# Six of eight chunks of an MLP up projection computed as Strassen products of quarters

## The chip, the cores and the metric

The kernel runs on one core of one Trainium2 chip. The metric is the device time of one execution in microseconds (us). TensorE does the matmuls, VectorE, ScalarE and GpSimd the elementwise work, and SyncE issues loads. The engines run side by side and wait for each other through semaphores.

## The reference, cut to what matters

The program computes one layer of an encoder: a mixer, a cross-attention and a squared-ReLU MLP. All but the MLP's first half is left as it is.

```
D_MODEL, SEQ, D_FF = 2048, 512, 8192
def squared_relu_mlp(h, w_up, w_down):
    u = jax.nn.relu(jnp.einsum('bsd,df->bsf', h, w_up))
    return jnp.einsum('bsf,fd->bsd', u * u, w_down)
...
x = x + squared_relu_mlp(rms_norm(x, ln_mlp), w_mlp_up, w_mlp_down)
```

## The kernel before

All matmuls are in pairs of fp32r parts: a value is `hi` (rounded on ScalarE) plus `lo` (the rest, by a subtraction on VectorE), and a product of two values is three matmuls, hi by hi, hi by lo, lo by hi (`hi_lo`, lines 867 to 869).

The up projection of the MLP has D_FF = 8192 columns, in 64 slabs of 128 columns, eight to a chunk (`MC`), eight chunks (`NCH`). A slab is 2048x128 weights: 1 MB, held as 128x2048 in `w_raw`, two buffers. Its 16 blocks of 128x128 are the stationary operand, the 512 tokens of `act_hi` and `act_lo` the moving one: 16 x 3 matmuls of 512 columns into one bank `slab_ps` (`window`). SyncE loads `w_raw` as soon as the split of the slab two before is done. ScalarE makes `w_hi` (`split_hi`, L1491), VectorE `w_lo` (`split_lo`, L2096). After a slab VectorE takes the ReLU and scales it (`hidden_relu`, L2792, into `urelu`), ScalarE squares it into `ucomb` (`hidden_square`, L1962). After two slabs GpSimd makes four sums of 128x256 out of the squares (`sum_hidden`, L813 to L816: the down projection is already done as Strassen products, and these are its activation sums). ScalarE and VectorE split the seven operands (`u_hi` L1970, `u_lo` L2799, 128x1792), and GpSimd's queue parks both in DRAM (`park_hidden`, `u_park`). In slabs 1 to 4 of the first chunk TensorE also transposes `main`, the residual, 16 blocks in each (`main_turns`, L1428), and ScalarE and VectorE copy them back.

Every engine's queue is in the order in which its code is written (`up_chunk` on ScalarE and on VectorE, `window` on TensorE, `sum_hidden` and `park_hidden` on GpSimd), and an instruction that waits holds up all behind it. Chunks 1 to 6 are a loop. Then the down projection follows, with `half_hi` (L2008) and `half_lo` (L2834) as its weight splits and `t` as its weight sums, all 128x1024.

## Time and profile before

| | |
|---|---|
| time, three executions | 2875.32, 2876.81, 2878.39 us, median 2876.81 |
| span of the profiled execution | 2873.9 us, from its first to its last instruction |
| the profiled execution's own time | not given apart from its span |
| busy: TensorE, VectorE, ScalarE, GpSimd | 2837.2, 1653.3, 1060.7, 405.2 us |
| ReLUs of the up projection, first and last | 1553.8 and 2245.0 us of the span |

A busy time counts the span from the start to the modelled end of an engine's instructions. Matmuls are pipelined, so that the time of one as shown is longer than the distance from its start to the next one's; the distance is what a row of them costs. Ends on VectorE and ScalarE overlap the next start a little too. An instruction's idle time before it stands in brackets, with what ended it.

### The profile page before, as it was taken

What the parts mean: (1) busy time and instruction counts of PE and PEld (TensorE: products, weight loads), DVE (VectorE), ACT (ScalarE), POOL (GpSimd) and SP (SyncE); (2) the same over time, 40 slices, a digit from 0 to 9 for tenths busy, and PEclk for the clock granted to TensorE, in tenths of its full rate; (3) what the DMA queues carried; (4) which work ended last, traced back from release to release, by engine and by line L of the source; (5) the groups of instructions that cost most, each with busy time, mean ns of one, the idle gap of its engine ahead of it and who ended that gap; (6) DMA issues with size and microseconds to landing.
All of it is one profiled execution on the core that took longest, in us unless ns stands there. A gap on an engine that the chain in (4) does not pass through costs nothing.

```text
span 2873.9 us, 38425 instructions
## 1 busy us (share of the span) xinstructions
PE 2837.2 (99%) x14896; PEld 2372.4 (83%) x14896; DVE 1653.3 (58%) x1699; ACT 1060.7 (37%) x1155; POOL 405.2 (14%) x438
## 2 busy tenths in 40 slices
PE   8999999999999999999999999999999999999997
PEld 5888777788899988898888888888888888888886
DVE  7545777755454433534534433333343798888888
ACT  5433433423453322332424322323233333333334
POOL 4000000000001132200011233233233200000001
PEclk9999999999999999999999999999999999999999
DMA  5333232233357764423423555556556755556555
GB/s 166 97 85 87 75 82 63 68 91 81 107 145 233 218 201 121 176 88 105 145 74 88 165 184 186 177 174 195 179 166 203 270 219 219 208 215 218 205 211 132
DMA packets 453647, 439.80 MB, mean 153 GB/s; under 512 B 9104, under 2 KB 365488, under 8 KB 453424
## 3 DMA queue, kind: packets, MB, share of 16 engines
q1 hardware_dynamic: 424288, 344.56, 39.1%
q0 software_dynamic: 29264, 93.90, 9.2%
q8 instruction: 68, 1.11, 0.2%
...
## 4 chain that ended last, share of the span: by engine, by line
PE 89%; DVE 5%; ACT 2%; DMA 2%; issue 2%; POOL 0%; DVEq 0%; SPq 0%; ACTq 0%
PE slab_ps L867 18%; PE slab_ps L869 18%; PE slab_ps L868 18%; PE down_ps L1465 6%; PE down_ps L1467 6%; PE down_ps L1466 6%; PE mix_ps L869 2%; PE mix_ps L868 2%; PE mix_ps L867 2%; PE down_ps L867 2%; PE down_ps L869 2%; PE down_ps L868 2%; DVE dn_c L2246 1%; ACT w_hi L1491 1%; DMA w_raw<-in_w_in_dram 1%
## 5 line engine op out<-in xcount | busy, mean ns | idle before, releaser
L867 PE MATMUL slab_ps<-act_hi,w_hi 128*128 128x512 f32 (+2 forms) x2704 | 1022.6, 378 | 15.1 <-DVE act_lo L2148 11.2
L868 PE MATMUL slab_ps<-act_lo,w_hi 128*128 128x512 f32 (+2 forms) x2704 | 999.8, 370 | 0.0
L869 PE MATMUL slab_ps<-act_hi,w_lo 128*128 128x512 f32 (+2 forms) x2704 | 999.8, 370 | 0.0
L2096 DVE TENSOR_TENSOR w_lo<-w_raw,w_hi 128x2048 fp32r<-128x2048 f32 x200 | 469.2, 2346 | 370.7 <-ACT w_hi L1491 370.0
L867 PEld LDWEIGHTS slab_ps<-act_hi,w_hi 128*128 128x128 f32 (+1 forms) x2704 | 509.5, 188 | 109.6 <-issue 23.4
L869 PEld LDWEIGHTS slab_ps<-act_hi,w_lo 128*128 128x128 f32 (+1 forms) x2704 | 509.2, 188 | 87.9 <-issue 0.8
L868 PEld LDWEIGHTS slab_ps<-act_lo,w_hi 128*128 128x128 f32 (+1 forms) x2704 | 509.8, 189 | 85.0 <-issue 5.1
L1491 ACT ACTIVATE w_hi<-w_raw 128x2048 fp32r<-128x2048 f32 x200 | 381.9, 1910 | 476.1 <-PE slab_ps L869 359.8
L1465 PE MATMUL down_ps<-half_hi,u_slot 128*128 128x512 f32 x896 | 349.5, 390 | 0.8 <-DMA u_slot<-u_park 0.8
L1467 PE MATMUL down_ps<-half_lo,u_slot 128*128 128x512 f32 x896 | 349.5, 390 | 0.0
L1466 PE MATMUL down_ps<-half_hi,u_slot 128*128 128x512 f32 x896 | 349.3, 390 | 0.0
L1962 ACT ACTIVATE ucomb<-urelu 128x512 f32<-128x512 f32 x64 | 40.5, 633 | 485.0 <-DVE urelu L2792 485.0
L2008 ACT ACTIVATE half_hi<-t 128x1024 fp32r<-128x1024 f32 x128 | 135.7, 1062 | 208.9 <-PE down_ps L1467 159.0
L1465 PEld LDWEIGHTS down_ps<-half_hi,u_slot 128*128 128x128 f32 x896 | 168.3, 188 | 36.9 <-issue 1.2
L2792 DVE SCALAR_TENSOR_TENSOR urelu<-slab_ps,rstd 128x512 f32<-128x512 f32 x64 | 44.3, 692 | 268.1 <-PE slab_ps L869 264.8
L1466 PEld LDWEIGHTS down_ps<-half_hi,u_slot 128*128 128x128 f32 x896 | 168.3, 188 | 35.7
L1467 PEld LDWEIGHTS down_ps<-half_lo,u_slot 128*128 128x128 f32 x896 | 168.3, 188 | 35.6
L2834 DVE TENSOR_TENSOR half_lo<-t,half_hi 128x1024 fp32r<-128x1024 f32 x128 | 157.3, 1230 | 13.8 <-ACT half_hi L2008 12.8
L2008 ACT ACTIVATE half_hi<-b 128x1024 fp32r<-128x1024 f32 x96 | 101.8, 1063 | 149.6 <-PE down_ps L1467 146.1
L2834 DVE TENSOR_TENSOR half_lo<-b,half_hi 128x1024 fp32r<-128x1024 f32 x96 | 117.1, 1221 | 6.5 <-ACT half_hi L2008 6.5
L2101 DVE TENSOR_TENSOR stage<-slab_ps,rstd 128x512 f32<-128x512 f32 (+1 forms) x56 | 38.6, 690 | 111.3 <-PE slab_ps L869 111.1
L2880 DVE TENSOR_TENSOR main<-main,down_ps 128x1024 f32<-128x1024 f32 x64 | 78.1, 1220 | 25.5 <-PE down_ps L1467 25.5
...
## 6 DMA issues: line engine op xcount, KB each, us to landing
w_raw<-in_w_mlp_up_dram SPq DMA_DIRECT2D x64, 1024.0 KB, 6.7
b<-in_w_mlp_down_dram SPq DMA_DIRECT2D x64, 1024.0 KB, 6.9
w_raw<-in_w_in_dram SPq DMA_DIRECT2D x56, 1024.0 KB, 5.6
...
w_raw<-in_w_cross_kv_dram SPq DMA_DIRECT2D x32, 1024.0 KB, 6.3
u_park<-u_hi POOLq DMA_DIRECT2D x32, 896.0 KB, 9.0
u_park<-u_lo POOLq DMA_DIRECT2D x32, 896.0 KB, 8.9
w_raw<-in_w_mix_out_dram SPq DMA_DIRECT2D x16, 1024.0 KB, 5.8
```

What stands on the lines that cost most here:

```text
L867: mm(ps, wh, xh, start=first, stop=False)
L868: mm(ps, wh, xl, start=False, stop=False)
L869: return mm(ps, wl, xh, start=False, stop=last)
L1465: mm(bank[:, t], uh, wh[:, j], start=first, stop=False)
L1466: mm(bank[:, t], ul, wh[:, j], start=False, stop=False)
L1467: ins = mm(bank[:, t], uh, wl[:, j], start=False, stop=last)
L1491: fn(w_hi[:, slot], w_raw[:, slot], ACT.Copy).then_inc(on["slab_hi"], 1)
L2008: fn(half_w[0][h % 4][:], source[q][:, 2 * half:2 * half + 2], ACT.Copy).then_inc(on["slab_hi"], 1)
L2096: tt(w_lo[:, slot], w_raw[:, slot], f32(w_hi[:, slot]), ALU.subtract).then_inc(on["slab_lo"], 1)
L2792: stt(out=urelu[w % 2][:], in0=G[(slabs.first - 1) % 2][:], scalar=0.0, in1=rstd[:], op0=ALU.max, op1=ALU.mult).then_inc(on["slab_out"], 1)
L2834: tt(half_w[1][h % 4][:], source[q][:, 2 * half:2 * half + 2], f32(half_w[0][h % 4][:]), ALU.subtract).then_inc(on["slab_lo"], 1)
L2880: tt(acc[n][q_], acc[n][q_], blocks(bank), ALU.add).then_inc(on["slab_out"], 1)
```

## The change

Chunks 1 to 6 of the up projection are computed in pairs of slabs. The 2048x256 weights of a pair are four quarters of 1024x128 (`b11`, `b12`, `b22`, `b21`, by half of the rows and slab), the activations four quarters of 1024 by 256 tokens. Seven products of one weight operand and one activation operand (`LEFT`) take the place of eight: each 8 x 3 matmuls of 256 columns, added up in three half banks (`joint`, `inner`, `top`).

- SyncE loads four quarters of 512 KB for a pair (`next_quarters`), each as its buffer is freed.
- VectorE makes four weight sums of 128x1024 in a pair (`first_weight_sum` to `fourth_weight_sum`), and seven `w_lo` of 128x1024 (`weight_lo`). ScalarE makes the seven `w_hi` (`weight_hi`). `w_hi` and `w_lo` are rings of four.
- ScalarE copies the bank out after four of the seven products (`part_out`), VectorE adds the parts and takes the ReLU (one operation of 512 columns, five of 256), ScalarE squares. One of the two halves has its sign turned around, and takes the minimum with zero.
- The activation operands are made once, in the first chunk: `left_parts` (ten operations of 128x2048 on VectorE in all) and `left_hi`, `left_lo`, four each. Two of the operands lie where `main` was, so `main` is parked in DRAM before and loaded again in the last chunk, and the transposes move to slabs 3 to 6 of the last chunk. A third lies in a quarter of `act_hi` and `act_lo`; that quarter is parked and loaded again behind product 4 of the last pair, and `returned_window`, the first slab after the pairs, takes its other half first.
- GpSimd's sums of the squares and the parking stay as they are, in numbers and sizes. They lag one pair behind and use one half of `ucomb`, because `t_raw` and one `b12_raw` take the other.

```diff
+        quarter_act = lambda t, i, j: t[:, KT // 2 * j:KT // 2 * (j + 1), HS * i:HS * (i + 1)]
+        ring = lambda w, n: w[:, 1 - n % 4 // 2, n % 2 * (SLAB // 2):(n % 2 + 1) * (SLAB // 2)]
+        LEFT = ([quarter_act(t, 0, 0) for t in (act_hi, act_lo)], [s1[:, part] for part in range(2)],
+                [s24[:, 0, part] for part in range(2)], [s24[:, 1, part] for part in range(2)],
+                [quarter_act(t, 1, 0) for t in (act_hi, act_lo)], [quarter_act(t, 0, 1) for t in (act_hi, act_lo)],
+                [quarter_act(t, 1, 1) for t in (act_hi, act_lo)])
+        left_sum = t1[:].rearrange("p j (a t) -> p (j a) t", t=HS)
+        b11_raw, b22_raw, b21_raw = w_raw[:, 1, 0:SLAB // 2], w_raw[:, 0, 0:SLAB // 2], w_raw[:, 0, SLAB // 2:SLAB]
+        t_raw = ucomb[:, 1, 0:4].rearrange("p a t -> p (a t)")
+        b12_raw = (w_raw[:, 1, SLAB // 2:SLAB], ucomb[:, 1, 4:8].rearrange("p a t -> p (a t)"))
+        weight_raw = lambda n: (b11_raw, t_raw, t_raw, b22_raw, b12_raw[n // STN % 2], b21_raw, t_raw)[n % STN]
+        st_banks = lambda j: (M[j % 2][:, 0:HS], M[2 + j % 2][:, 0:HS], M[4 + j % 2][:, 0:HS])
...
+            def next_quarters(c, j):
+
+                src = quarter_of(c, j + 1, 0, 0)
+                sp.wait_ge(on["slab_lo"], c * (STN * HM) + (ST0 + STN * j + 1))
+                load_quarter(b11_raw, src, raw_in[1])
+                src = quarter_of(c, j + 1, 0, 1)
+                if past_first(c, j > 0):
+                    sp.wait_ge(on["slab_lo"], c * (STN * HM) + (ST0 + STN * (j - 1) + 5))
+                else:
+                    sp.wait_ge(on["u_lo_done"], HM - 1)
+                load_quarter(b12_raw[(j + 1) % 2], src, x_loaded[1])
+                src = quarter_of(c, j + 1, 1, 1)
+                sp.wait_ge(on["slab_lo"], c * (STN * HM) + (ST0 + STN * j + 5))
+                load_quarter(b22_raw, src, raw_in[0])
+                src = quarter_of(c, j + 1, 1, 0)
+                sp.wait_ge(on["slab_lo"], c * (STN * HM) + (ST0 + STN * j + 7))
+                load_quarter(b21_raw, src, x_loaded[0])
...
-            with pe.Fori(1, NCH) as c:
-                slabs.enter(c - 1, MC)
-                for _ in range(MC):
-                    window()
-            slabs.leave(NCH - 1)
+
+            def strassen_pair(c, j):
+
+                joint, inner, top = st_banks(j)
+                for i in range(STN):
+                    n = STN * j + i
+                    pe.wait_ge(on["slab_lo"], c * (STN * HM) + (ST0 + n + 1))
+                    if i == 0 and past_first(c, j >= 2):
+                        pe.wait_ge(on["slab_out"], c * (STN * HM) + (ST0 + STN * j - STN))
+                    if i in (2, 3, 4, 6):
+                        pe.wait_ge(st_copied, c * (4 * HM) + (COPY0 + 4 * j + {2: 1, 3: 2, 4: 3, 6: 4}[i]))
+                    if isinstance(c, int) and c == 0 and j == 0:
+                        if i == 0:
+                            pe.wait_ge(on["x_rstd"], 2)
+                        if i in (1, 2, 3, 4):
+                            pe.wait_ge(on["act_ready"], i + (5 * KT))
+                    wh, wl = (ring(w, n).rearrange("p (k n) -> p k n", n=P) for w in (w_hi, w_lo))
+                    xh, xl = LEFT[i]
+                    bank = (joint, inner, joint, inner, joint, top, joint)[i]
+                    for k in range(KT // 2):
+                        first, end = k == 0 and i in (0, 1, 5), k == KT // 2 - 1
+                        mm(bank, wh[:, k], xh[:, k], start=first, stop=False, skip_group_check=True)
+                        mm(bank, wh[:, k], xl[:, k], start=False, stop=False, skip_group_check=True)
+                        last = mm(bank, wl[:, k], xh[:, k], start=False, stop=end, skip_group_check=True)
+                    last.then_inc(on["slab_mul"], 1)
+
...
+            def left_hi(i):
+                act.wait_ge(st_sums, i + LEFT0)
+                fn(LEFT[i][0], left_sum, ACT.Copy).then_inc(on["xg_hi"], 1)
...
+            def weight_hi(c, n):
+
+                i, j = n % STN, n // STN
+                p = c * HM + (j + 1)
+                if past_first(c, n >= 4):
+                    act.wait_ge(on["slab_mul"], c * (STN * HM) + (ST0 + n - 3))
+                if i in (0, 3, 5):
+                    act.wait_ge({0: raw_in[1], 3: raw_in[0], 5: x_loaded[0]}[i], 16 * p + (16 if i == 5 else RAW0))
+                elif i == 4:
+                    act.wait_ge(st_sums, 4 * (p) + (SUMS0 - 1))
+                elif i == 6:
+                    act.wait_ge(st_sums, 4 * (p) + (SUMS0 - 0))
+                elif i == 1:
+                    act.wait_ge(st_sums, 4 * (p) + (SUMS0 - 3))
+                else:
+                    act.wait_ge(st_sums, 4 * (p) + (SUMS0 - 2))
+                fn(ring(w_hi, n), weight_raw(n), ACT.Copy).then_inc(on["slab_hi"], 1)
...
+            def strassen_pair(c, j, last=False):
+
+                joint, inner, top = st_banks(j)
+                n = STN * j
+                weight_hi(c, n + 3)
+                act.wait_ge(on["u_squared"], c * (2 * HM) + 2 * (HM + j))
+                part_out(c, n, urelu0[:, 0:HS], joint)
+                weight_hi(c, n + 4)
+                part_out(c, n + 1, urelu1[:, HS:S], inner)
+                weight_hi(c, n + 5)
+                part_out(c, n + 2, urelu1[:, 0:HS], joint)
+                weight_hi(c, n + 6)
+                act.wait_ge(on["u_summed"], c * HM + (HM + j))
+                act.wait_ge(on["u_hi_parked"], c * (16 * HM) + 16 * (HM - 1 + j))
+                fn(u_hi[:], ucomb[:, 0, 1:], ACT.Copy).then_inc(on["u_hi_done"], 1)
+                if not last:
+                    weight_hi(c, n + 7)
+                part_out(c, n + 4, urelu0[:, HS:S], joint)
+                if last:
+                    slabs.step(STN * PAIRS - 1)
+                    split_hi(NOT_SLABS, slabs.at(-1))
                     slabs.step()
+                else:
+                    weight_hi(c, n + 8)
+                    weight_hi(c, n + 9)
+                pair_square(c, j, 1)
+                pair_square(c, j, 0)
 
             up_chunk(0, first=True)
-            with act.Fori(1, NCH - 1) as c:
-                slabs.enter(c - 1, MC)
-                up_chunk(c)
-            slabs.leave(NCH - 2)
...
+            def left_parts(i):
+
+                h, l = ([f32(quarter_act(t, *at)) for at in ((0, 0), (0, 1), (1, 0), (1, 1))] for t in (act_hi, act_lo))
+                negated = lambda t: stt(out=left_sum, in0=left_sum, scalar=-1.0, in1=t, op0=ALU.mult, op1=ALU.subtract)
+                plus, minus = ((lambda a, b, op=op: tt(left_sum, a, b, op)) for op in (ALU.add, ALU.subtract))
+                if i == 1:
+                    chain.link(minus(h[3], h[2]))
+                    chain.link(plus(left_sum, l[3]))
+                    minus(left_sum, l[2]).then_inc(st_sums, 1)
+                elif i in (2, 3):
+                    dve.wait_ge(on["act_ready"], i - 1 + (5 * KT))
+                    at = 0 if i == 2 else 1
...
+            def left_lo(i):
+                dve.wait_ge(on["xg_hi"], i + (5 * KT))
+                tt(LEFT[i][1], left_sum, f32(LEFT[i][0]), ALU.subtract).then_inc(on["act_ready"], 1)
...
+                            v.tensor_copy(main[:, 4 * w - 16:4 * w - 12, t * P:(t + 1) * P],
+                                          M[2 + t][:].rearrange("p (k d) -> p k d", d=P)).then_inc(on["main_odd"], 1)
                     if w % 2 and not (first and w == 1):
                         hidden_lo(c, (w - 3) // 2)
+                    if first:
+                        if w in (2, 3, 4):
+                            left_lo(w - 1)
+                        if w <= 4:
+                            left_parts(w)
+                    if not (first and w == MC - 1):
+                        slabs.step()
...
+            def weight_lo(c, n):
+                dve.wait_ge(on["slab_hi"], c * (STN * HM) + (ST0 + n + 1))
+                tt(ring(w_lo, n), weight_raw(n), f32(ring(w_hi, n)), ALU.subtract).then_inc(on["slab_lo"], 1)
...
+            def fourth_weight_sum(c, j):
+
+                dve.wait_ge(x_loaded[0], c * (16 * HM) + 16 * (j + 1) + 16)
+                dve.wait_ge(on["slab_lo"], c * (STN * HM) + (ST0 + STN * j + 3))
+                tt(t_raw, t_raw, b21_raw, ALU.add).then_inc(st_sums, 1)
+
+            def strassen_pair(c, j, last=False):
+
+                joint, inner, top = st_banks(j)
+                n = STN * j
+                product = lambda i: dve.wait_ge(on["slab_mul"], c * (STN * HM) + (ST0 + n + i + 1))
+                copied = lambda i: dve.wait_ge(st_copied, c * (4 * HM) + (COPY0 + 4 * j + i))
+                upper, lower = slice(0, HS), slice(HS, S)
+                third_weight_sum(c, j)
+                weight_lo(c, n + 3)
+                weight_lo(c, n + 4)
+                weight_lo(c, n + 5)
+                fourth_weight_sum(c, j)
+                weight_lo(c, n + 6)
+                dve.wait_ge(on["u_hi_done"], c * HM + (HM + j))
+                dve.wait_ge(on["u_lo_parked"], c * (16 * HM) + 16 * (HM - 1 + j))
+                tt(u_lo[:], ucomb[:, 0, 1:], f32(u_hi[:]), ALU.subtract).then_inc(on["u_lo_done"], 1)
+                product(3)
+                copied(3)
+                tt(urelu1[:, upper], inner, urelu1[:, upper], ALU.add).then_inc(on["slab_out"], 1)
+                if not last:
+                    first_weight_sum(c, j + 1)
+                    weight_lo(c, n + 7)
+                    weight_lo(c, n + 8)
+                    second_weight_sum(c, j + 1)
+                copied(4)
+                tt(urelu1[:, lower], urelu0[:, lower], urelu1[:, lower], ALU.add).then_inc(st_middle, 1)
+                dve.wait_ge(on["slab_out"], c * (STN * HM) + (ST0 + STN * j + 1))
+                dve.wait_ge(st_middle, c * HM + (MID0 + j + 1))
+                stt(out=urelu1[:], in0=urelu1[:], scalar=0.0, in1=rstd[:], op0=ALU.min, op1=ALU.mult).then_inc(
+                    st_relu, 1)
+                if last:
+                    slabs.step(STN * PAIRS - 1)
+                    split_lo()
                     slabs.step()
+                else:
+                    weight_lo(c, n + 9)
+                product(5)
+                tt(urelu0[:, upper], top, urelu0[:, upper], ALU.add).then_inc(on["slab_out"], 1)
+                dve.wait_ge(on["slab_out"], c * (STN * HM) + (ST0 + STN * j + 2))
+                stt(out=urelu0[:, upper], in0=urelu0[:, upper], scalar=0.0, in1=rstd[:, upper], op0=ALU.max,
+                    op1=ALU.mult).then_inc(st_relu, 1)
+                product(6)
+                stt(out=urelu0[:, lower], in0=joint, scalar=0.0, in1=rstd[:, lower], op0=ALU.max, op1=ALU.mult).then_inc(
```

The places in the queues that this moves. On VectorE, the rows of two slabs were these (taken from the last chunk, where the rows of the loop over chunks 1 to 6 stand in the same order, without the loop's register rows between):

```order
L2792 SCALAR_TENSOR_TENSOR urelu<-slab_ps,rstd 128x512
L2096 TENSOR_TENSOR w_lo<-w_raw,w_hi 128x2048
L2799 TENSOR_TENSOR u_lo<-ucomb,u_hi 128x1792
L2792 SCALAR_TENSOR_TENSOR urelu<-slab_ps,rstd 128x512
L2096 TENSOR_TENSOR w_lo<-w_raw,w_hi 128x2048
```

And now chunks 1 to 6 have this for a pair (12 of 18 rows, from the pairs written out ahead of the loop; ahead of them stand the third sum and three `w_lo`, behind them two more ReLU rows):

```order
L3107 TENSOR_TENSOR ucomb<-ucomb,w_raw 128x1024
L3077 TENSOR_TENSOR w_lo<-ucomb,w_hi 128x1024
L3124 TENSOR_TENSOR u_lo<-ucomb,u_hi 128x1792
L3127 TENSOR_TENSOR urelu<-mix_ps,urelu 128x256
L3088 TENSOR_TENSOR ucomb<-w_raw,ucomb 128x1024
L3077 TENSOR_TENSOR w_lo<-w_raw,w_hi 128x1024
L3077 TENSOR_TENSOR w_lo<-ucomb,w_hi 128x1024
L3094 TENSOR_TENSOR ucomb<-ucomb,w_raw 128x1024
L3134 TENSOR_TENSOR urelu<-urelu 128x256
L3137 SCALAR_TENSOR_TENSOR urelu<-urelu,rstd 128x512
L3077 TENSOR_TENSOR w_lo<-ucomb,w_hi 128x1024
L3146 TENSOR_TENSOR urelu<-mix_ps,urelu 128x256
```

One `urelu` row and one `w_lo` row for each slab, and one `u_lo` row for two, have become seventeen shorter rows and `u_lo`; the row L3107 (the fourth sum) and the `w_lo` row that splits it stand one behind the other.

On VectorE in the first chunk, from the split of slab 2 on, before:

```order
L2096 TENSOR_TENSOR w_lo<-w_raw,w_hi 128x2048
L2792 SCALAR_TENSOR_TENSOR urelu<-slab_ps,rstd 128x512
L2096 TENSOR_TENSOR w_lo<-w_raw,w_hi 128x2048
L2811 COPY main<-mix_ps 128x4x128 x2
L2792 SCALAR_TENSOR_TENSOR urelu<-slab_ps,rstd 128x512
L2096 TENSOR_TENSOR w_lo<-w_raw,w_hi 128x2048
```

And now, where `t` is `left_sum` and `s` one of the operands that `left_lo` makes:

```order
L2323 TENSOR_TENSOR w_lo<-w_raw,w_hi 128x2048
L3032 TENSOR_TENSOR t<-act_hi 128x2048
L3032 TENSOR_TENSOR t<-t,act_lo 128x2048 x2
L3019 SCALAR_TENSOR_TENSOR urelu<-slab_ps,rstd 128x512
L2323 TENSOR_TENSOR w_lo<-w_raw,w_hi 128x2048
L3050 TENSOR_TENSOR s<-t,s 128x2048
L3031 SCALAR_TENSOR_TENSOR t<-t,act_hi 128x2048
L3032 TENSOR_TENSOR t<-t,act_lo 128x2048
L3019 SCALAR_TENSOR_TENSOR urelu<-slab_ps,rstd 128x512
L2323 TENSOR_TENSOR w_lo<-w_raw,w_hi 128x2048
L3026 TENSOR_TENSOR u_lo<-ucomb,u_hi 128x1792
```

The copies of transposed blocks (L2811) are gone from here, and between one 128x2048 `w_lo` and the next stand sums of the same size.

On ScalarE in the first chunk, before:

```order
L1491 ACTIVATE w_hi<-w_raw 128x2048
L1962 ACTIVATE ucomb<-urelu 128x512
L1491 ACTIVATE w_hi<-w_raw 128x2048
L1982 ACTIVATE main<-mix_ps 128x4x128 x2
L1962 ACTIVATE ucomb<-urelu 128x512
L1491 ACTIVATE w_hi<-w_raw 128x2048
```

And now:

```order
L1638 ACTIVATE w_hi<-w_raw 128x2048
L2121 ACTIVATE s<-t 128x2048
L2109 ACTIVATE ucomb<-urelu 128x512
L1638 ACTIVATE w_hi<-w_raw 128x2048
L2121 ACTIVATE s<-t 128x2048
L2109 ACTIVATE ucomb<-urelu 128x512
L1638 ACTIVATE w_hi<-w_raw 128x2048
```

A row `s<-t` (`left_hi`, which waits for the last of VectorE's sums) stands ahead of the next square and the next `w_hi`.

## Rows read from the trace of the kernel before

**Rows 1.** The page: parts 1 and 2, then 4

```profile
PE 2837.2 (99%) x14896; PEld 2372.4 (83%) x14896; DVE 1653.3 (58%) x1699; ACT 1060.7 (37%) x1155; POOL 405.2 (14%) x438
...
PEclk9999999999999999999999999999999999999999
...
PE 89%; DVE 5%; ACT 2%; DMA 2%; issue 2%; POOL 0%; DVEq 0%; SPq 0%; ACTq 0%
```

**Rows 2.** Timeline of TensorE (start, us, instruction): 52 of 256 columns; 15 of 512

```profile
939.80 0.28 PE L869 MATMUL slab_ps<-act_hi,w_lo 128*128 128x256 f32 x1
...
945.92 0.28 PE L869 MATMUL slab_ps<-act_hi,w_lo 128*128 128x256 f32 x1
...
1559.73 0.39 PE L867 MATMUL slab_ps<-act_hi,w_hi 128*128 128x512 f32 x1
...
1562.91 0.39 PE L869 MATMUL slab_ps<-act_hi,w_lo 128*128 128x512 f32 x1
```

**Rows 3.** Timeline of VectorE over two slabs in the loop

```profile
1646.67 0.69 DVE L2792 SCALAR_TENSOR_TENSOR urelu<-slab_ps,rstd 128x512 f32<-128x512 f32 x1 [5.02 <-PE slab_ps L869]
1649.95 2.29 DVE L2096 TENSOR_TENSOR w_lo<-w_raw,w_hi 128x2048 fp32r<-128x2048 f32 x1 [2.59 <-ACT w_hi L1491]
1652.16 2.02 DVE L2799 TENSOR_TENSOR u_lo<-ucomb,u_hi 128x1792 fp32r<-128x1792 f32 x1
...
1660.66 2.64 DVE L2096 TENSOR_TENSOR w_lo<-w_raw,w_hi 128x2048 fp32r<-128x2048 f32 x1 [2.50 <-ACT w_hi L1491]
1668.43 0.69 DVE L2792 SCALAR_TENSOR_TENSOR urelu<-slab_ps,rstd 128x512 f32<-128x512 f32 x1 [5.13 <-PE slab_ps L869]
```

**Rows 4.** Timeline of VectorE and ScalarE in the down projection

```profile
2411.14 1.22 DVE L2834 TENSOR_TENSOR half_lo<-b,half_hi 128x1024 fp32r<-128x1024 f32 x1
...
2412.28 1.22 DVE L2859 TENSOR_TENSOR t<-b 128x1024 f32<-128x1024 f32 x1
...
2412.64 1.06 ACT L2008 ACTIVATE half_hi<-b 128x1024 fp32r<-128x1024 f32 x1 [1.66 <-PE down_ps L1467]
...
2413.73 1.23 DVE L2834 TENSOR_TENSOR half_lo<-b,half_hi 128x1024 fp32r<-128x1024 f32 x1 [0.23 <-ACT half_hi L2008]
```

**Rows 5.** Groups by form: count, busy us, mean ns of one, idle before

```profile
L2614 DVE TENSOR_TENSOR kv_t<-slab_ps,mem_r 128x256 f32<-128x256 f32 x32 | 13.6, 424 | 34.1 <-PE slab_ps L869 34.0
```

**Rows 6.** Timeline of ScalarE in the same two slabs

```profile
1647.49 0.63 ACT L1962 ACTIVATE ucomb<-urelu 128x512 f32<-128x512 f32 x1 [8.51 <-DVE urelu L2792]
1648.03 1.90 ACT L1491 ACTIVATE w_hi<-w_raw 128x2048 fp32r<-128x2048 f32 x1
1649.83 1.69 ACT L1970 ACTIVATE u_hi<-ucomb 128x1792 fp32r<-128x1792 f32 x1
```

**Rows 7.** Timeline of GpSimd beside the split at 1660.66

```profile
1660.41 0.74 POOL L815 TENSOR_TENSOR ucomb<-ucomb 128x256 f32<-128x256 f32 x1
1661.23 2.67 POOL L816 TENSOR_TENSOR ucomb<-ucomb 128x256 f32<-128x256 f32 x1
```

**Rows 8.** Timeline of VectorE, then GpSimd, at the seam to the down projection

```profile
2247.33 3.29 DVE L2834 TENSOR_TENSOR half_lo<-t,half_hi 128x1024 fp32r<-128x1024 f32 x2 [1.65 <-ACT half_hi L2008]
2250.54 1.75 DVE L2853 TENSOR_TENSOR t<-b,t 128x1024 f32<-128x1024 f32 x1
...
2247.93 1.60 POOL L815 TENSOR_TENSOR ucomb<-ucomb 128x256 f32<-128x256 f32 x1
2249.61 1.60 POOL L816 TENSOR_TENSOR ucomb<-ucomb 128x256 f32<-128x256 f32 x1
```

**Rows 9.** Timeline of VectorE, then TensorE, in the first chunk

```profile
1557.02 2.29 DVE L2096 TENSOR_TENSOR w_lo<-w_raw,w_hi 128x2048 fp32r<-128x2048 f32 x1 [2.50 <-ACT w_hi L1491]
...
1563.14 1.91 PE L1428 MATMUL mix_ps<-ident,main 128*128 128x128 f32 x16
```

**Rows 10.** The page, part 6: issues, KB each, median us to landing

```profile
w_raw<-in_w_mlp_up_dram SPq DMA_DIRECT2D x64, 1024.0 KB, 6.7
...
u_park<-u_hi POOLq DMA_DIRECT2D x32, 896.0 KB, 9.0
```

More of the change, by code:

```diff
@@ L522, in quarter @@
+            load_freed(1)
+            sp.wait_ge(on["slab_mul"], done + 5 + ST0)
+            for part, t in enumerate((act_hi, act_lo)):
+                sp.dma_start(quarter_act(t, 1, 0).bitcast(F32), left_park[part]).then_inc(on["x_in2"], 16)
+            for j in range(2, MC):
+                load(w_last(j))
             def quarter(dst, c, n, f_half, n_half, sem):
@@ new lines, in _, with returned_window @@
+            for j in range(HM):
+                strassen_pair(0, j)
+            with pe.Fori(1, STC) as c:
+                for j in range(HM):
+                    strassen_pair(c, j)
+            def returned_window():
+                slot = slabs.first % 2
+                pe.wait_ge(on["slab_lo"], slabs.at(1))
+                wh, wl = (w[:, slot].rearrange("p (k n) -> p k n", k=KT) for w in (w_hi, w_lo))
+                for i in range(KT):
+                    k = (i + KT // 2) % KT
+                    if k == 0:
+                        pe.wait_ge(on["x_in2"], 32 + 16)
+                    last = hi_lo(G[slot][:], wh[:, k], wl[:, k], act_hi[:, k], act_lo[:, k], i == 0, i == KT - 1)
+                last.then_inc(on["slab_mul"], 1)
+                slabs.step()
@@ L2819, in _ @@
+            for j in range(HM):
+                strassen_pair(STC - 1, j, j == HM - 1)
+            dve.wait_ge(on["u_squared"], (NCH - 1) * MC)
+            up_chunk(NCH - 1, last=True)
             dve.wait_ge(on["main_even"], 2 * NT)
```

224 lines of the change are left out of this document (174 added, 50 removed).

## Prediction

> **What bounds the kernel now.** I read the page first. TensorE is busy 2837.2 of 2873.9 us, the granted clock is 9 tenths or more in every slice (the 2.4 GHz level), and TensorE has 89% of the chain that ended last [rows 1]. A microsecond of TensorE removed is a microsecond won, as long as the engines that feed it keep up. VectorE is busy 58% over the whole, but that average is of stages with different limits, so I went to the timeline of the up projection. Its matmuls start 0.227 us apart (14 intervals in 3.18 us), and the 256-column matmuls of an earlier stage start 0.120 us apart (51 in 6.12 us) [rows 2]. The ReLU of one slab and that of the next but one start 21.76 us apart, so a slab costs 10.88 us, which is 48 x 0.227: TensorE never waits [rows 3]. ScalarE and VectorE work for some 4 us of each slab and then idle for the matmuls. This is the stage that changes.
>
> **What the products cost TensorE.** A pair of slabs was 2 x 16 x 3 = 96 matmuls of 512 columns, 21.76 us. It becomes 7 x 8 x 3 = 168 of 256 columns: 168 x 0.120 = 20.16 us. That is 1.60 us less, not one eighth of 21.76 (2.72), since a 256-column matmul costs 0.120 and not 0.1135. Six chunks of four pairs are 24 pairs: 38.4 us less, if nothing else binds.
>
> **What the products cost VectorE.** In one pair it now issues 11 operations of 128x1024 (seven weight splits, four sums), `u_lo` of 128x1792, one operation of 512 columns and five of 256. Back to back, a 128x1024 one starts 1.14 us after the one before (2411.14, 2412.28; I take 1.135, the mean over a longer stretch), though it is shown as 1.22 [rows 4]: ends overlap by 0.08. In the same way `u_lo` takes 2.02 - 0.08 = 1.94 and the 512-column one 0.69 - 0.08 = 0.61 [rows 3], a 256-column one 0.42 - 0.08 = 0.34 [rows 5]. Sum: 12.49 + 1.94 + 0.61 + 1.70 = 16.74 us. This fits under 20.16, so it doesn't bind by itself. But its queue is in order, and each weight split waits for ScalarE's half of it, which for six of seven waits for a sum or a product. I laid one pair end to end over both queues, with 0.04 us from an end to the start it releases (half_hi ends 2413.70, half_lo starts 2413.73 [rows 4]):
> - ReLU of product 6, then the square (0.63 - 0.09 = 0.54 [rows 6]) and the first split of the next pair (1.06 [rows 4]) on ScalarE, while VectorE has 0.34 + 1.135 to do: it waits 0.61.
> - Fourth sum, then split on ScalarE: 1.22 + 0.04 + 1.06 + 0.03 against 1.135: it waits 1.21. Nothing stands between the two in VectorE's queue.
> - `u_hi` (1.69 [rows 6]) starts behind that split on ScalarE: VectorE waits another 0.47.
> - Six places where it waits for its own last operation or a split just begun, 0.08 to 0.14 each: 0.71.
> Waits: 3.00 us. Together 19.74, still under 20.16.
>
> **What GpSimd adds.** The four sums of the hidden activations now run beside a VectorE that has little idle time. The trace shows what that costs. The weight split that starts while GpSimd's third sum runs takes 2.64 instead of 2.29 us [rows 3], and the fourth sum, issued behind it, 2.67 instead of 0.74 [rows 7]. At the seam to the down projection both engines have work waiting: two 128x1024 operations take 3.29 us together instead of 2.35, the next 1.75 instead of 1.22, and the GpSimd sums in between 1.60 each [rows 8]. So each GpSimd sum costs a waiting VectorE 0.47 to 0.53. In a pair the first falls into VectorE's 0.61 us wait, the other three cost 0.34 + 0.47 + 0.47 = 1.28. VectorE's round is 16.74 + 3.00 + 1.28 = **21.02 us**. It is longer than TensorE's 20.16, so it sets the pace, and TensorE waits 0.87 us in each pair, at product 2, whose bank ScalarE copies late. ScalarE itself has about 11 us in a pair: seven splits, `u_hi`, two squares, four copies of 256 columns.
>
> The Trainium skill, SBUF — State Buffer, section Who interferes with whom, has the rule: a VectorE instruction with two SBUF inputs and a GpSimd one that reads SBUF exclude each other, and the second waits for the end of the first. It speaks against this change, which takes away the idle time in which GpSimd ran. For GpSimd the trace agrees (2.67 behind a 2.29 us split, 1.60 behind a 1.22 us one). For VectorE a rule taken to the letter would charge the whole sum, the trace charges 0.47 to 0.53; the sum here goes by the trace, the letter is a rival below.
>
> Gain of the pairs: 24 x 21.02 = 504.5, and about 0.8 more in the first two, where the split of `left_sum` for product 4 and late weights come on top, so 505.3 against 24 x 21.76 = 522.2: **-16.9 us**. Bounds: GpSimd's hold at 0.35 (2.64 - 2.29 [rows 3]) gives a round of 20.70, -24.6; longer handovers (0.12 for 0.04) and a hold of 0.54 give 21.6, -3.
>
> **The first chunk.** It loses the transposes of `main` (four times 16, 1.9 us each [rows 9]) and the last chunk gets them: nothing. It gets `left_parts`, ten sums of 128x2048, three `left_lo` and three `left_hi` beside its slabs. Alone that would fit, but in the queues they stand between one weight split and the next. From the split's start at 1557.02 [rows 9], the same in both kernels: split 2.21, three chained sums 6.95, then on ScalarE `left_hi` 1.82, square 0.54, `w_hi` 1.90, with handovers: the next split starts at 1570.5. From there 2.21 + 0.7 (GpSimd) + `left_lo` 2.21 + two sums 4.66 + the same 4.36 on ScalarE: 1584.6, done 1587.0, while slab 4 is due at 1563.14 + 2 x 10.88 = 1584.9. It waits 2.1. The next turn has `u_lo` too: slab 5 waits 4.8. The one after has three sums: slab 6 waits 4.0. Together **+11 us** (8 to 14, as the chained sums take 2.25 to 2.40 each).
>
> **The return to whole slabs.** Product 4 of the last pair frees the quarter of `act_hi` and `act_lo` that has to come back from `left_park`: 2 MB, behind 1 MB of weights in the same queue, beside `u_park`. 1 MB lands 6.7 us after its issue, and 0.9 MB of `u_park` 9.0 [rows 10]. They are wanted 5.8 + 5.4 us after the issue. I estimate 15 us for them all, a wait of **+4 us** once (1 to 9). The loads of the quarters themselves have 12 us or more between the split that frees a buffer and the sum that reads it, against 6.7 for twice the bytes: nothing. So has the parking of `main`. If that cover were gone, one late quarter in each pair would cost what it is late times 24. The two joins of `acc` that move behind the last chunk (1.22 each) lie in VectorE's idle time of its last slab, 10.88 less about 7.
>
> **Sum.** -16.9 + 11 + 4 = -1.9 us. The profiled execution has a span of 2873.9, which would be 2872.0; its own time isn't given apart, and the median of the three runs, 2876.8, is 2.9 above the span. **Predicted: 2875 us.** What a measurement of this kernel can tell from no change is about 0.2%, 5.8 us.
>
> **Rivals.**
> - *TensorE stays the bound (9%).* If GpSimd's sums cost VectorE nothing, the round is 19.7 and 20.16 holds: 24 x 1.60 = -38.4, +2 at the start, +15: -21, 2855 us. For it: VectorE's own sum of 16.74. Against it: [rows 7, 8].
> - *A shorter round or shorter stalls (17%).* Hold 0.35, first chunk 8, return 2: about -11 and less, 2862 to 2870 us.
> - *A longer round (20%).* The short operations wait for registers and semaphores at more places than I count; 0.4 to 0.6 us in a pair give 2882 to 2889 us.
> - *The whole GpSimd sum is charged (6%), slower.* Three times 0.73 in place of 1.28 makes 21.9: 24 x 0.9 = +21, 2896 us. For it: 0.73 is what such a sum takes alone. Against it: [rows 8]. The pairs win nothing from a hold of about 0.7 on. The Trainium skill's rule (SBUF — State Buffer, Who interferes with whom), to the letter, would be this case.
> - *`u_hi` waits for GpSimd (5%), slower.* From the square, the four sums have 8.1 us until ScalarE wants them; at 0.73 + 3 x 1.6 they take about 6. At 2.67 each [rows 7] they take 10.7, 2.6 us too long in each pair: +62, 2936 us. Against it: 2.67 belongs to a 2.29 us split ahead, and here they are 1.22 long.
> - *The forecast (43%)*, 2870 to 2881 us.
>
> The cases of the wrong sign hold nearly as much as those of the right, and a change of nothing is the likeliest. Faster by over 0.2% takes the first two and a little of the third: 0.30. Slower takes the longer round, the two GpSimd cases: 0.30. The range leaves out the first and the two GpSimd rivals, 20% together: 2862 to 2889 us.
>
> **What would show it.** Right: pairs 21.0 us apart in the loop, a TensorE wait of some 0.9 us at one product in seven, VectorE's largest waits before the split behind the fourth sum and before `u_lo`; GpSimd's sums at 1.2 to 1.6 us; three TensorE waits of 2 to 5 us before slabs 4, 5 and 6 for `w_lo`, and one within the first slab of the last chunk for the returned quarter. Wrong: pairs at 20.2 us (the port costs nothing), at 21.8 or above (nothing is won in the pairs), a TensorE wait for a loaded quarter, or a first chunk without waits.

## The result and the profile after

The changed kernel takes **2891.24 us** (median of 4 runs, 2890.13 to 2894.06), the kernel before 2876.15 us on the same chip (2875.32 to 2878.39). The ratio is 1.0054, with a 95% interval of 1.0039 to 1.0068. The forecast was 2875 us, no change, with a range up to 2889: the result lies 2 us above the range, and on the side of slower.

The page of the changed kernel, parts 1, 2 and 4, which answers to [rows 1]:

```profile
span 2888.5 us, 42880 instructions
...
PE 2809.0 (97%) x16624; PEld 2426.2 (84%) x16624; DVE 1944.7 (67%) x2025; ACT 1177.0 (41%) x1375; POOL 431.6 (15%) x448
...
PEclk9999999999999999999999999999999999999999
...
PE 73%; DVE 12%; ACT 5%; issue 5%; DMA 3%; DVEq 0%; SPq 0%; POOL 0%; ACTq 0%
```

TensorE did get less work: 2809.0 us busy instead of 2837.2. But the span is 14.6 us longer, so TensorE idles for 42.8 us more, and its share of the chain that ended last fell from 89% to 73%. VectorE took the largest part of what it lost. The waits of TensorE say where (what waits, for what: us in total, times, longest):

```profile
PE mix_ps L1556 <- ACT urelu L2165: 25.4, 23, 1.4
...
PE slab_ps L967 <- DVE w_lo L2323: 10.6, 5, 4.5
PE slab_ps L967 <- DMA act_lo<-left_park: 6.4, 1, 6.4
```

These are the three places that the prediction named: one wait of 1.1 us in each pair of slabs (0.87 was forecast), the waits of the first chunk (three of them, 9.0 us; the other two are not in this stage), and the returned quarter.

I then laid the ReLUs of both traces side by side. The stage's first ReLU starts at 1553.82 us before and 1554.19 after, its last at 2244.99 and 2259.28, 14.3 us later. The ReLU of the first chunk's last slab, before and then now (timelines of VectorE):

```profile
1635.81 0.69 DVE L2792 SCALAR_TENSOR_TENSOR urelu<-slab_ps,rstd 128x512 f32<-128x512 f32 x1 [1.29 <-PE slab_ps L869]
...
1640.53 0.69 DVE L3019 SCALAR_TENSOR_TENSOR urelu<-slab_ps,rstd 128x512 f32<-128x512 f32 x1 [0.83 <-PE slab_ps L969]
```

- **First chunk.** That ReLU starts 4.7 us later. 0.4 of it are there at the stage's first ReLU already, and 7.1 us of transposes have left: the chunk itself takes +11.4 us.
- **24 pairs.** TensorE's matmuls of them take 515.1 us (1640.3 to 2155.4), and 522.2 before: 7.1 us less, where 16.9 less was forecast. A pair is 21.37 us in the loop and 21.53 where the first and last chunk are written out.
- **Return.** Within the next slab the matmuls stand still from 2160.78 to 2167.56, 6.5 us more than from one to the next, the slow clock (below) takes 2.8, and the first matmuls of the slab 0.2: +9.5 us. The 7.1 us of transposes are in the last four slabs, 12.65 us each.

One steady pair of the changed kernel, on VectorE (timeline), which answers to [rows 3]:

```profile
1881.45 0.42 DVE L3151 SCALAR_TENSOR_TENSOR urelu<-mix_ps,rstd 128x256 f32<-128x256 f32 x1
1881.78 1.22 DVE L3101 TENSOR_TENSOR ucomb<-ucomb,w_raw 128x1024 f32<-128x1024 f32 x1
1883.51 1.23 DVE L3077 TENSOR_TENSOR w_lo<-w_raw,w_hi 128x1024 fp32r<-128x1024 f32 x1 [0.51 <-ACT w_hi L2161]
1884.73 1.69 DVE L3077 TENSOR_TENSOR w_lo<-ucomb,w_hi 128x1024 fp32r<-128x1024 f32 x1
1886.34 1.75 DVE L3077 TENSOR_TENSOR w_lo<-w_raw,w_hi 128x1024 fp32r<-128x1024 f32 x1
1888.02 1.75 DVE L3107 TENSOR_TENSOR ucomb<-ucomb,w_raw 128x1024 f32<-128x1024 f32 x1
1890.89 1.23 DVE L3077 TENSOR_TENSOR w_lo<-ucomb,w_hi 128x1024 fp32r<-128x1024 f32 x1 [1.12 <-ACT w_hi L2161]
1892.58 2.03 DVE L3124 TENSOR_TENSOR u_lo<-ucomb,u_hi 128x1792 fp32r<-128x1792 f32 x1 [0.46 <-ACT u_hi L2191]
...
1902.82 0.42 DVE L3151 SCALAR_TENSOR_TENSOR urelu<-mix_ps,rstd 128x256 f32<-128x256 f32 x1
```

The three waits in brackets stand where the prediction put them, with 0.51, 1.12 and 0.46 us. Three operations of the same size as the 1.22 us ones take 1.69, 1.75 and 1.75. GpSimd says why (timeline, the same pair), which answers to [rows 8]:

```profile
1882.62 0.96 POOL L899 TENSOR_TENSOR ucomb<-ucomb 128x256 f32<-128x256 f32 x1 [7.75 <-ACT ucomb L2174]
1883.54 1.79 POOL L900 TENSOR_TENSOR ucomb<-ucomb 128x256 f32<-128x256 f32 x1
1885.41 1.60 POOL L901 TENSOR_TENSOR ucomb<-ucomb 128x256 f32<-128x256 f32 x1
1887.09 1.60 POOL L902 TENSOR_TENSOR ucomb<-ucomb 128x256 f32<-128x256 f32 x1
```

Each of VectorE's three long operations lies beside a sum of GpSimd's, and each of those is longer than the 0.74 us that it takes alone.

In the first chunk and at the return the waits are followed by slow matmuls, which the prediction did not have. The first matmuls behind each of the two longest waits (timeline of TensorE), which answer to [rows 2]:

```profile
1603.29 0.79 PE L967 MATMUL slab_ps<-act_hi,w_hi 128*128 128x512 f32 x1 [4.53 <-DVE w_lo L2323]
1603.88 0.63 PE L968 MATMUL slab_ps<-act_lo,w_hi 128*128 128x512 f32 x1
1604.30 0.63 PE L969 MATMUL slab_ps<-act_hi,w_lo 128*128 128x512 f32 x1
...
2160.78 0.39 PE L969 MATMUL slab_ps<-act_hi,w_lo 128*128 128x512 f32 x1
2167.56 0.80 PE L967 MATMUL slab_ps<-act_hi,w_hi 128*128 128x512 f32 x1 [6.39 <-DMA act_lo<-left_park]
2168.15 0.63 PE L968 MATMUL slab_ps<-act_lo,w_hi 128*128 128x512 f32 x1
```

They start 0.43 us apart instead of 0.227 [rows 2]. The windows around both, with one over the first returned slab (length, busy time and count of each engine, granted clock, DMA share, GB/s):

```profile
1602.00:1608.00 6.00, 4.71 (x14) 3.78 (x15) 5.96 (x3) 0.00 (x0) 1.82 (x1) 0.72 0.53 137
2166.00:2174.00 8.00, 6.44 (x17) 5.05 (x18) 0.00 (x0) 0.00 (x0) 0.00 (x0) 0.57 1.06 273
2155.41:2176.02 20.61, 14.22 (x50) 11.15 (x50) 3.62 (x4) 2.44 (x2) 4.82 (x4) 0.83 0.95 294
```

The granted clock is 0.57 in the second: the engine came out of the wait at its 1.2 GHz level and was at 2.4 GHz again some 6 us later. The page's row of 40 slices can't show it, since a slice is 72 us. At the return it costs 2.8 us, since the next slab waits for nothing. In the first chunk slab 5 is 1.7 us slower for it, and yet this costs nothing: slab 6 waits for its `w_lo` whenever slab 5 is done, and what slab 5 loses comes off that wait. The first ReLU of the stage and the start of slab 6, in the changed kernel and then in one with short GpSimd sums (below), show it:

```profile
1554.19 0.69 DVE L3019 SCALAR_TENSOR_TENSOR urelu<-slab_ps,rstd 128x512 f32<-128x512 f32 x1 [3.30 <-ACT rstd L1654]
1618.40 0.50 PE L967 MATMUL slab_ps<-act_hi,w_hi 128*128 128x512 f32 x1 [2.36 <-DVE w_lo L2323]
...
1555.28 0.69 DVE L3028 SCALAR_TENSOR_TENSOR urelu<-slab_ps,rstd 128x512 f32<-128x512 f32 x1 [3.30 <-ACT rstd L1663]
1619.52 0.50 PE L976 MATMUL slab_ps<-act_hi,w_hi 128*128 128x512 f32 x1 [1.06 <-DVE w_lo L2332]
```

It is 64.2 us from one to the other in both, though slow matmuls take TensorE 1.9 us beyond their usual time in the first and 4.8 in the second.

### The profile page after: what moved, and what is told of

Its sections match the earlier page's. It is cut to its first block, busy times and chain, and to the rows that moved or that the text cites. A ratio compares the mean times of both kernels' runs of the same rounds, so it can differ in the third digit from the quotient of the medians.

```text
span 2888.5 us, 42880 instructions
## 1 busy us (share of the span) xinstructions
PE 2809.0 (97%) x16624; PEld 2426.2 (84%) x16624; DVE 1944.7 (67%) x2025; ACT 1177.0 (41%) x1375; POOL 431.6 (15%) x448
## 3 DMA queue, kind: packets, MB, share of 16 engines
q8 instruction: 78, 1.28, 0.2%
## 4 chain that ended last, share of the span: by engine, by line
PE 73%; DVE 12%; ACT 5%; issue 5%; DMA 3%; DVEq 0%; SPq 0%; POOL 0%; ACTq 0%
PE slab_ps L967 12%; PE slab_ps L969 11%; PE slab_ps L968 11%; PE down_ps L1610 6%; PE down_ps L1612 6%; PE down_ps L1611 6%; DVE w_lo L3077 4%; PE mix_ps L969 2%; PE mix_ps L968 2%; PE mix_ps L967 2%; PE down_ps L967 2%; PE down_ps L969 2%; PE down_ps L968 2%; ACT w_hi L2161 2%; PE mix_ps L1556 1%
## 5 line engine op out<-in xcount | busy, mean ns | idle before, releaser
L967 PE MATMUL slab_ps<-act_hi,w_hi 128*128 128x512 f32 (+2 forms) x1936 | 726.4, 375 | 31.1 <-DVE act_lo L2375 11.4
L968 PE MATMUL slab_ps<-act_lo,w_hi 128*128 128x512 f32 (+2 forms) x1936 | 702.8, 363 | 0.0
L969 PE MATMUL slab_ps<-act_hi,w_lo 128*128 128x512 f32 (+2 forms) x1936 | 702.5, 363 | 0.0
L967 PEld LDWEIGHTS slab_ps<-act_hi,w_hi 128*128 128x128 f32 (+1 forms) x1936 | 366.4, 189 | 97.8 <-issue 24.2
L969 PEld LDWEIGHTS slab_ps<-act_hi,w_lo 128*128 128x128 f32 (+1 forms) x1936 | 366.1, 189 | 58.6 <-issue 0.8
L968 PEld LDWEIGHTS slab_ps<-act_lo,w_hi 128*128 128x128 f32 (+1 forms) x1936 | 366.8, 189 | 55.1 <-issue 5.1
L1558 PE MATMUL mix_ps<-act_hi,w_lo 128*128 128x256 f32 x768 | 217.3, 283 | 0.0
L1556 PE MATMUL mix_ps<-act_hi,w_hi 128*128 128x256 f32 x768 | 217.3, 283 | 0.0
L1557 PE MATMUL mix_ps<-act_lo,w_hi 128*128 128x256 f32 x768 | 217.3, 283 | 0.0
L1556 PE MATMUL mix_ps<-s,w_hi 128*128 128x256 f32 x576 | 164.8, 286 | 26.7 <-ACT urelu L2165 25.4
L1557 PE MATMUL mix_ps<-s,w_hi 128*128 128x256 f32 x576 | 162.4, 282 | 0.0
```

What stands on the lines that cost most here:

```text
L967: mm(ps, wh, xh, start=first, stop=False)
L968: mm(ps, wh, xl, start=False, stop=False)
L969: return mm(ps, wl, xh, start=False, stop=last)
L1556: mm(bank, wh[:, k], xh[:, k], start=first, stop=False, skip_group_check=True)
L1557: mm(bank, wh[:, k], xl[:, k], start=False, stop=False, skip_group_check=True)
L1558: last = mm(bank, wl[:, k], xh[:, k], start=False, stop=end, skip_group_check=True)
```

## The experiments

**Theory A** is the prediction's: VectorE's round, its own work with its waits and with GpSimd's holds (a hold is the time by which a GpSimd sum lengthens VectorE's work), sets the pace of the pairs. **Theory B**, the rival, takes the page's largest wait at its word: TensorE waits for ScalarE's copy of a bank (L2165), so ScalarE's order sets it.

**The copy ahead of a split (against B).** In a pair's ScalarE code:

```diff
-                weight_hi(c, n + 3)
                 act.wait_ge(on["u_squared"], c * (2 * HM) + 2 * (HM + j))
                 part_out(c, n, urelu0[:, 0:HS], joint)
+                weight_hi(c, n + 3)
```

> On ScalarE, in each pair, the copy of product 0 out of its bank goes ahead of the first weight split of the pair. Theory A (VectorE's round with its waits for ScalarE sets the pace, 21.4 us a pair, and TensorE's wait for the copy only shows it): the copy comes 1 us earlier, the split 0.3 us later, and so the round is 0.2 to 0.3 us longer; TensorE's wait moves from product 2 to another one or to a weight split; +5 to +7 us, 2896 to 2898 us. Theory B (the copy of the bank is what TensorE's one wait of 1.1 us in a pair is for, and it sets the pace): the wait goes, pairs 20.3 us apart, -24 us, 2867 us.

Measured: 2893.22 us (2891.15 to 2895.24); the median is 2 us above the changed kernel's, and the runs of the two overlap. B falls, since nothing was won. The copy now starts 1.19 us behind the start of VectorE's last ReLU of a pair and not 1.93, but TensorE's wait for it is still the largest entry and did not get shorter, because what is late is VectorE (timeline):

```profile
PE mix_ps L1556 <- ACT urelu L2165: 25.4, 23, 1.2
...
1884.69 1.22 DVE L3101 TENSOR_TENSOR ucomb<-ucomb,w_raw 128x1024 f32<-128x1024 f32 x1
1886.91 1.36 DVE L3077 TENSOR_TENSOR w_lo<-w_raw,w_hi 128x1024 fp32r<-128x1024 f32 x1 [1.00 <-ACT w_hi L2161]
...
1891.55 1.21 DVE L3107 TENSOR_TENSOR ucomb<-ucomb,w_raw 128x1024 f32<-128x1024 f32 x1
```

Its first wait of the pair grew from 0.51 to 1.00 us. In the trace the round grew by only 0.09 us, since everything behind that wait moved against GpSimd's sums and the fourth weight sum came clear of them (1.21 instead of 1.75). A's size (5 to 7 us) missed that, its sign was right.

**The fourth sum one split earlier (for A).** In a pair's VectorE code:

```diff
                 weight_lo(c, n + 4)
-                weight_lo(c, n + 5)
                 fourth_weight_sum(c, j)
+                weight_lo(c, n + 5)
                 weight_lo(c, n + 6)
```

> On VectorE, in each pair, the fourth weight sum goes one place forward, ahead of the split of product 5, so that this split lies between the sum and the split that ScalarE has to start from it. Theory A: VectorE's wait of 1.12 us behind the fourth sum and most of the 0.46 us before u_lo go, its round falls from 21.4 to 19.9 us, TensorE's 20.16 sets the pace: 24 x 1.2 = -28 us, 2863 us, and TensorE waits for nothing in the loop. Theory B: the copy of product 0 comes as late as before, pairs stay 21.4 us apart, 2891 us.

Measured: 2861.6 us (2858.31 to 2861.89), ratio to the kernel before 0.9947 (0.993 to 0.9963). One moved line gives 29.6 us back, and the kernel is now faster than before. The same place of a pair on VectorE (timeline):

```profile
1849.36 2.90 DVE L3077 TENSOR_TENSOR w_lo<-w_raw,w_hi 128x1024 fp32r<-128x1024 f32 x2 [0.52 <-ACT w_hi L2161]
1852.18 1.76 DVE L3107 TENSOR_TENSOR ucomb<-ucomb,w_raw 128x1024 f32<-128x1024 f32 x1
1853.87 1.75 DVE L3077 TENSOR_TENSOR w_lo<-w_raw,w_hi 128x1024 fp32r<-128x1024 f32 x1
1855.54 1.21 DVE L3077 TENSOR_TENSOR w_lo<-ucomb,w_hi 128x1024 fp32r<-128x1024 f32 x1
1857.15 2.03 DVE L3124 TENSOR_TENSOR u_lo<-ucomb,u_hi 128x1792 fp32r<-128x1792 f32 x1 [0.39 <-ACT u_hi L2191]
```

The wait of 1.12 us behind the sum is gone: ScalarE's split of that sum now has VectorE's next split as its cover. The windows of two pairs show the new bound, the second pair of chunk 2 and a later one:

```profile
1748.14:1767.84 19.70, 19.70 (x166) 19.58 (x165) 18.94 (x20) 11.13 (x14) 7.90 (x6) 1.00 0.67 206
...
1887.48:1907.57 20.09, 20.09 (x170) 20.09 (x169) 19.16 (x20) 11.25 (x14) 8.01 (x6) 1.00 0.66 197
```

TensorE is busy throughout in both. In the first, and the two pairs after it, VectorE's round is 19.7 us while it catches up with TensorE; from there on the pair is 20.09 us, TensorE's 168 matmuls at 0.120 (20.16). So TensorE is the bound again. The step from 21.37 to 19.70 is the wait of 1.12 us and half a microsecond of smaller waits that I did not take apart. GpSimd's holds are still there.

**GpSimd's sums cut short.** In chunks 1 to 6 the four sums of the hidden activations take 8 of their 256 columns (they leave out the rest of those sums, so the operands of the down projection aren't formed):

```diff
-                    sum_hidden(c * HM + (HM - 1 + j), 0)
+                    short_hidden(c * HM + (HM - 1 + j), 0)
...
+                a21, a11, a22, a12, s1, s2, s3, s4 = (ucomb[:, buf, n, 0:8] for n in range(PROD + 1))
```

> Leaves out most of the hidden activations' sums: beside chunks 1 to 6 GpSimd's four sums take 8 of 256 columns; all else is as in the changed kernel. Theory A with the price of the port: the three holds of 0.47 to 0.54 us in a pair go, the round is 19.9 us, pairs come at 20.2 us, about 2863 us. Theory A without a price of the port (VectorE's operations are long there for another reason): pairs stay at 21.4 us and the weight splits at 1.7 us. Theory B: 21.4 us too, but with short splits.

Measured: one run, 2857.71 us. The pair is 19.9 to 20.1 us, TensorE's bound. Its timeline, VectorE and then GpSimd:

```profile
1849.47 2.45 DVE L3086 TENSOR_TENSOR w_lo<-w_raw,w_hi 128x1024 fp32r<-128x1024 f32 x2 [0.51 <-ACT w_hi L2170]
1852.10 1.23 DVE L3086 TENSOR_TENSOR w_lo<-w_raw,w_hi 128x1024 fp32r<-128x1024 f32 x1 [0.19 <-ACT w_hi L2170]
1853.24 1.22 DVE L3116 TENSOR_TENSOR ucomb<-ucomb,w_raw 128x1024 f32<-128x1024 f32 x1
1855.59 1.23 DVE L3086 TENSOR_TENSOR w_lo<-ucomb,w_hi 128x1024 fp32r<-128x1024 f32 x1 [1.13 <-ACT w_hi L2170]
...
1848.98 0.20 POOL L909 TENSOR_TENSOR ucomb<-ucomb 128x8 f32<-128x8 f32 x1
```

The wait behind the fourth sum is as long as ever, 1.13 us, and all four operations take 1.22 to 1.23. The long ones of the changed kernel are GpSimd's doing, shown by taking its work away. With the holds gone the round is 21.37 - 1.56 = 19.8 us, with the wait gone 19.7: it takes both to lift VectorE's round above TensorE's.

**The quarter reloaded first.** On SyncE, the reload of `left_park` goes ahead of the second load of weights, and GpSimd's reload of `main` comes one slab later:

```diff
-            sp.wait_ge(on["slab_lo"], done + 7 + ST0)
-            load_freed(1)
             sp.wait_ge(on["slab_mul"], done + 5 + ST0)
...
+            sp.wait_ge(on["slab_lo"], done + 7 + ST0)
+            load_freed(1)
```

> The quarter of act_hi and act_lo that comes back is loaded ahead of the second slab's weights of the last chunk, and the first half of main is loaded one slab later. Theory A (the quarter waits behind other transfers, and TensorE's 6.6 us wait also costs the slow clock behind it, 3 us): the wait falls to 2 us or less, the matmuls behind it are 0.227 us apart and not 0.43, -7 us, 2884 us. Rival (2 MB take 12 us by themselves, whatever stands ahead): the wait stays above 5 us, -1 us, 2890 us.

Measured: 2890.13 us (2888.85 to 2891.29), 1.1 us less than the changed kernel. TensorE's wait went from 6.4 to 5.1 us, and the last ReLU of the stage came 1.8 us earlier counted from the first. The order in the queue is a small part of the wait; the rival was nearer.

**The quarter in two halves.** The same, with the quarter read back as two times four k tiles, and TensorE waiting for each half when it comes to it:

```diff
-            for part, t in enumerate((act_hi, act_lo)):
-                sp.dma_start(quarter_act(t, 1, 0).bitcast(F32), left_park[part]).then_inc(on["x_in2"], 16)
+            for half, sem in enumerate(("x_in2", "x_in3")):
+                ks = slice(KT // 4 * half, KT // 4 * (half + 1))
+                for part, t in enumerate((act_hi, act_lo)):
+                    sp.dma_start(quarter_act(t, 1, 0)[:, ks].bitcast(F32), left_park[part][:, ks]).then_inc(on[sem], 16)
```

> The changed kernel with the parked left quarter read back ahead of the load of w_raw (as in the return-first kernel, 2890.1 us), GpSimd's reloads of the main activations one slab later, and the quarter read back as two halves of four k tiles with a semaphore each, so that TensorE starts on the first while the second is under way. Theory A (the wait is for the 2 MB to land, and a wait of this length costs TensorE's clock as well: 5.1 us waited and about 1.8 us lost at the 1.2 GHz level in the return-first kernel): the wait becomes about 2.5 us and the slow matmuls go with it, 2886 (2884 to 2887.5). Theory B (both halves land together, since their packets share the same 16 engines; only the issue is split): 2889 to 2891. Theory C (the time is lost again at a later slab, whose weights come later): 2889 to 2891 with a w_lo wait one or two slabs on.

Measured: 2891.36 us (2890.81 to 2892.9), nothing won. Theory C held. Two lines of TensorE's timeline:

```profile
2166.69 0.50 PE L969 MATMUL slab_ps<-act_hi,w_hi 128*128 128x512 f32 x1 [3.17 <-DMA act_lo<-left_park]
...
2174.52 0.80 PE L969 MATMUL slab_ps<-act_hi,w_hi 128*128 128x512 f32 x1 [3.23 <-DVE w_lo L2327]
```

The wait at the quarter is 2 us shorter, and a wait of 3.2 us for the next slab's weights has come up. The DMA engines are 0.95 busy over the returned slab of the changed kernel (the third window above) at 294 GB/s. While the quarter, the weights and `u_park` all want to land, an order only chooses which of them is late. The wait for the quarter and the one for weights behind it add up to 6.4 us in the changed kernel, 5.1 with the quarter first and 6.4 here. This is argued from these sums: no run left the other transfers out.

**ScalarE's order in the first chunk.** The high half of the next weights first, then a left quarter (one slab later than now), then the square:

```diff
-                    if w:
+                    if w and not first:
                         hidden_square(c, w - 1)
                     if w < MC - 1:
                         split_hi(NOT_SLABS if last else 0)
+                    if first and w in (2, 3, 4):
+                        if w == 3:
+                            act.wait_ge(on["x_parked"], 16 * KT + 64)
+                        left_hi(w - 1)
+                    if w and first:
+                        hidden_square(c, w - 1)
                     if w % 2 and not (first and w == 1):
                         hidden_hi(c, (w - 3) // 2)
-                    if first and w in (1, 2, 3):
-                        if w == 2:
-                            act.wait_ge(on["x_parked"], 16 * KT + 64)
-                        left_hi(w)
```

> The changed kernel with another order on ScalarE in the first chunk of the six alone: the high half of the next slab's weights is written first, then the high half of one left quarter, then the previous slab's ReLU is squared (left quarters one slab later than now). Theory A (the first chunk's loss of 11.8 us is ScalarE's order: the weights' high half stands behind a left quarter and a square, so the low half on VectorE and the slab are late, 9.5 us of waits and 2.2 us of slow clock): some 10 us come back, 2881 (2879 to 2884) against 2891.2 for the changed kernel, and TensorE's matmuls before slab 5 are 0.23 us apart throughout. Theory B (VectorE itself has too much to do in that chunk: the left sums and the low halves): the waits only move to VectorE's own rows, 2888 to 2892.

Measured: 2878.99 us (2877.51 to 2880.62, 10 runs), 12.2 us less than the changed kernel. Theory A held in the main: its size was a little low, and the slow clock in it was no loss of its own, as shown above. The first chunk from ReLU to ReLU (windows), the changed kernel's here and this one's in the next fence:

```profile
1554.19:1640.53 86.34, 77.30 (x332) 62.88 (x331) 60.37 (x33) 27.42 (x21) 22.15 (x20) 0.98 0.62 197
```

```profile
1554.25:1629.05 74.80, 74.80 (x332) 61.94 (x331) 61.26 (x33) 27.55 (x21) 29.97 (x20) 1.00 0.72 228
```

The same 332 matmuls take 11.54 us less, TensorE is busy in all of them, and the granted clock is 1.00. VectorE does the same 33 operations: it never had too much to do, its halves of the weights only stood behind ScalarE's. The edit changes both the order and the slab of a left quarter; which of the two is needed was not tried apart.

**All three together.** The fourth sum early, the first chunk's order, the quarter first.

> Three edits at once: VectorE's fourth weight sum one split earlier (2861.6 us alone), ScalarE's first chunk as in the first-chunk kernel, and the return first on SP (1.1 us alone). If the three places are independent: 2861.6 - 10 - 1.1 = 2850.5 (2848 to 2853), faster than the kernel before by 0.9%. Rival (the first chunk's time is given back: VectorE enters the pairs behind by what it saved in waits): 2857 to 2862.

Measured: **2847.26 us** (2845.39 to 2847.61, 4 runs), ratio to the kernel before 0.9897 (0.9881 to 0.9914). The three alone save 29.6, 12.2 and 1.1 us, 43.0 together; the kernel saves 44.0. The places are independent within 1 us, and this version beats both kernels.

**All three, with the halves.**

> As the kernel with all three edits, with the quarter read back in two halves. If the halves save 4 us by themselves: 2846.5 (2844 to 2849). If the halves land together: 2849 to 2852, no different from the kernel with three edits.

Measured: 2850.13 us (2847.67 to 2851.31), 2.9 us more than with the whole quarter. The wait at the quarter is 0.9 us, and one for weights is now 5.4. The halves are no use here either.

## Why the prediction was wrong

- **TensorE's cost of the products** (20.16 us for a pair): right. Where nothing holds it up a pair is 20.09 us.
- **What bounds the pairs** (VectorE's round, longer than TensorE's): right, shown by the copy and the fourth-sum kernels. The places and sizes of its waits were right: 0.61, 1.21 and 0.47 us forecast. Laid out from start to start in the rows above, beyond the occupancy of each operation (1.135 for a 128x1024 one), they are 0.60, 1.20 and 0.56.
- **What GpSimd adds: this step failed in size.** It said 0.34 + 0.47 + 0.47 = 1.28 us. From start to start it is 0.48 + 0.55 + 0.53 = 1.56. That is 0.28 of the 0.35 us by which the round of 21.02 was too short; the rest is `u_lo`'s wait (0.09) and roundings. The mistake was to take 0.34 for the first sum that meets VectorE, when the VectorE rows in [rows 8] showed 0.47 to 0.53 us for each sum. (Its cheap bound is off too: three holds of 0.35 make a round of 20.79, not 20.70.)
- **24 equal rounds.** The last chunk's and the first chunk's written-out pairs are 21.53 us, not 21.37, and one was 21.7: another 1.4 us. Together the pairs gave about 7 us and not 16.9. The bound of a longer round (21.6, -3) held them; the chosen value had a margin of 0.74 us over the before, so an error of 0.35 took away half of the gain.
- **The first chunk** (+11): right, 11.4. The waits before slabs 4, 5 and 6 were forecast 2.1, 4.8 and 4.0 us and were 2.3, 4.7 and 2.5. The third was smaller by the 1.7 us that slab 5 lost to the slow clock, which no term had: together 4.2. So this is no luck. Slab 6 starts when its `w_lo` is there, as forecast, whatever the clock did before.
- **The return** (+4, 1 to 9): this step failed too, +9.5. The wait was 6.5 us and not 4, and 2.8 us of slow clock came on top. The estimate of 15 us for the transfers was short: the quarter had landed 17.7 us after its first issue. It was put together from 6.7 us for 1 MB of weights and 9.0 for `u_park` [rows 10], and that 6.7 is a median of two kinds of loads. In the loop of the kernel before, loads that are issued beside the parks take 10.9 to 12.5 us, and the others 6.2 to 6.7 (`w_raw` from 1646 to 2157 us):

```profile
DMA to landing us min/median/max: 6.2/10.9/12.5
```

  At the return there were more transfers yet, and the window from the quarter's issue to its landing shows engines that are 0.94 busy:

```profile
2149.76:2167.56 17.80, 11.41 (x73) 9.95 (x71) 9.17 (x9) 5.26 (x5) 6.80 (x6) 0.97 0.94 303
```

- **The rivals.** The longer round came nearest: its range ended 2 us below the result, its 0.4 to 0.6 us in a pair were 0.35, and the cause was GpSimd's hold and not registers and semaphores. The whole GpSimd sum charged gives 21.9 us for a round, and it was 21.4: what VectorE pays is not the 1.6 us for which the two are entangled. The Trainium skill (SBUF — State Buffer, Who interferes with whom) has the two exclude each other, the second waiting for the end of the first. The rows agree on GpSimd's side, 1.60 us behind an operation that takes 1.22 alone; on VectorE's side they charge 0.47 to 0.55 of a sum that takes 0.74 alone, so the measurement decides. `u_hi` never waited for GpSimd.
- **The sum.** Errors of +9.8 (pairs), +0.4 (first chunk), +5.5 (return) and 0.4 ahead of the stage make 16.1, and the result was 16.2 above the forecast. All had one sign. The chosen values of the pairs and of the return stood nearer their cheap ends, and the range took its upper end from the pairs alone.
